# Two layers of each kind: five engine programs with a depth loop over a register, or written out one behind the other

## The chip, the cores and the metric

The kernel runs on one core of a Trainium2 chip. A core has five engines, each with its own instruction stream and its own sequencer: TensorE (PE; its weight loads are PEld), VectorE (DVE), ScalarE (ACT), GpSimd (POOL) and SyncE (SP), and 16 DMA engines that move data between device memory and on-chip memory. The engines meet only through semaphores: an instruction can wait until a semaphore has a value, and can raise one when it ends. The metric is the device time of one execution in microseconds; lower is better.

## The reference

A transformer of four layers on one sequence of 512 tokens with 1024 channels, in fp32: two layers of a first kind, then two of a second kind.

```python
def first_block(x, c, ...):
    c_act = silu(c)
    for l in range(DEPTH):                     # DEPTH = 2
        sh1, sc1, g1, sh2, sc2, g2 = split(c_act @ w_ada[l] + b_ada[l], 6)
        h = rms_norm(x, norm1_g[l]) * (1 + sc1) + sh1
        x = x + g1 * token_mixer(h, ...)       # gated linear attention + differential attention
        h = rms_norm(x, norm2_g[l]) * (1 + sc2) + sh2
        x = x + g2 * hier_moe(h, ...)          # 32 experts, 2 for each token
    return x

def second_block(x, ...):
    for l in range(DEPTH):
        h = _rmsnorm(x, norm1_g[l])
        q, k, v, su, sv, cb, cc, cx = split(h @ w_in[l])
        mix = concatenate([attention(rope(q), rope(k), v), spatial_gating(su, sv, sg_norm_g[l], ...), conv(cb, cc, cx)])
        x = x + mix @ w_out[l]
        h2 = _rmsnorm(x, norm2_g[l])
        gate, val = split(_dwconv3(h2 @ ffn_w_up[l], ffn_conv_w[l]))
        x = x + (silu(gate) * val) @ ffn_w_down[l]
    return x

def reference(...):
    return second_block(first_block(...), ...)
```

## The kernel before

Each engine has a program of its own: SyncE (line 570 on), GpSimd (677), TensorE (879), VectorE (1500) and ScalarE (2109). The five programs have the same shape. After a setup comes a loop over the two layers of the first kind, then one over the two layers of the second kind. These ten loops are `Fori(0, DEPTH)`: the layer `l` is a register, the body stands once in the instruction memory, and a branch at its end leads back. They begin at lines 615 and 647 (SyncE), 745 and 839 (GpSimd), 920 and 1277 (TensorE), 1520 and 1941 (VectorE), 2122 and 2340 (ScalarE).

The residual `xT` stays on chip, channels on the partitions. SyncE streams the weights into a ring of six slots of 4096 columns (`s_ring`). Matmuls with split weights run three times: ScalarE copies the high part of the weights and of the activations (`copy`, line 2112), GpSimd makes the low part of the weights (lines 767 and 860), VectorE the low part of the activations. All TensorE products are recorded by the helper `mm`, line 882. The small transfers of gains and tables are GpSimd's `small`, line 743. In the second half of each layer of the first kind, pairs of experts run in a second loop inside the first, over a number of pairs `ahead` that is read from memory (lines 641, 823, 1264, 1922, 2336). In a pass of it six transfers of 2048 KB bring the weights of two experts.

The order of work on each engine is that of its program, and the waits say how far the others must be. Every semaphore is counted up over the whole kernel: a helper `at(l, n)` gives the value for the n-th event of layer `l`, `l * per + n`. In a loop over a register that is a sum with a register in it, so a register step (ALU_OP in the trace, REGISTER_ALU in the compiled order) stands ahead of the instruction that waits. The engine's own chains are written with a helper too: `link` (lines 1945 to 1949) lets the next VectorE operation wait for the one before.

At the start of a layer of the second kind ScalarE squares the eight tiles of `xT` (line 2352), VectorE adds the squares one by one (`add_square`, below; its addition is line 1972, the register step of its wait line 1971), TensorE sums over the partitions with a matrix of ones, and the norm follows (lines 1955 to 1960). The layer ends with eight additions to `xT` on VectorE (line 2102), each released by a matmul.

```python
def add_square(squares, norm, k):
    ve.wait_ge(x_squared_b.sem, x_squared_b.at(l, KD * norm + k + 1))
    ins = ve.tensor_tensor(squares[0], squares[0], squares[k], ALU.add)
    if k < KD - 1:
        link(ins)
```

Of the kernel before, what the change touches and what calls it, by code (L numbers as in the profile page):

```python
# [39 lines left out]
DEPTH = 2  # L40
# [283 lines left out]
def program(nc, ctx, inp, out):  # L324
# [137 lines left out]
    def sig(name, per, credit=0):  # L462
        return Signal(sem(name), per, credit)
# [14 lines left out]
    linkA, linkB = sig("a_vector_link", LINKS["A"]), sig("b_vector_link", LINKS["B"])  # L478
# [18 lines left out]
    head_normed = sig("a_head_normed", 16)  # L497
# [52 lines left out]
    def settle(eng):  # L550

        eng.sem_inc(settled, 1)
# [4 lines left out]
    def slot_view(s, k, n):  # L557
        return ring[:, s, 0:k * n].rearrange("p (k n) -> p k n", k=k)
# [4 lines left out]
    def flat(units):  # L563
        return units.rearrange("p a s -> p (a s)")

    def tok(t, n=1):
        return slice(t * P, (t + n) * P)
# [4 lines left out]
    @block.sync  # L572
    def _(sp):
        def kn(w, c0, n):
            return w.rearrange("(k p) n -> p k n", p=P)[:, :, c0:c0 + n]


        for t in range(NT):
            sp.dma_start(flat(hT[:, 2 * t:2 * t + 2]), inp["x"][0, tok(t), :]).then_inc(x_in[t], 16)
        sp.wait_ge(cells_zero, 1)  # L580

        def source_a(name, l):
            kind, j = name[0], name[1] if len(name) > 1 else 0
            if kind == "ada":
                return KD, 512, kn(inp["w_ada"][l], 512 * j, 512)
            if kind == "lr":
                return KD, 32, kn(inp["w_in"][l], C_LR, 32)
            if kind in ("ya", "yb"):
                return 4, D, kn(inp["w_branch_a" if kind == "ya" else "w_branch_b"][l], 0, D)
            if kind == "wo":  # L590
                return KD, 512, kn(inp["w_out"][l], 512 * j, 512)
            c = {"gqk": 0, "gv": C_GV, "gg": C_GG, "dq": C_DQ, "dk": C_DK, "dv": C_DV, "ga": C_GA, "gb": C_GB}[kind]
            return KD, 512, kn(inp["w_in"][l], c + 512 * j, 512)

        freed_in_m = (m_in_read[0], m_in_read[1], m_down_made)

        last_of_high = {3: ("wo", 7), 4: ("wo", 3), 5: ("wo", 7)}

        def expert(l, number, e, u, layer_first, pieces=range(3)):

            for j in pieces:
                s = 3 * u + j
                if layer_first:

                    sp.wait_ge(TA.done.sem, TA.done_at(l, RA.reader_last(s) if s < 3 else last_of_high[s]))
                    settle(sp)

                sp.wait_ge(freed_in_m[j].sem, freed_in_m[j].at(number, u - 1))
                settle(sp)
                if j < 2:  # L610
                    sp.dma_start(slot_view(s, 4, D), kn(inp["w_expert_in"][l, e], 0, D)[:, 4 * j:4 * j + 4, :]).then_inc(weights_in_m[s], 16)
                else:
                    sp.dma_start(slot_view(s, 4, D), kn(inp["w_expert_out"][l, e], 0, D)).then_inc(weights_in_m[s], 16)

        with sp.Fori(0, DEPTH) as l:
            settle(sp)
            before = sp.value_load(cells[0:1, 0:1], min_val=0, max_val=BLOCKS)
            for name, *_ in RA.blocks:
                s = RA.slot(name)
                reader = RA.reader_before(name)  # L620
                if reader is None:

                    sp.wait_ge(freed_in_m[s % 3].sem, freed_in_m[s % 3].at(before * 2, s // 3 - 1))
                else:
                    sp.wait_ge(TA.done.sem, TA.done_at(l, reader))
                settle(sp)
                if name[0] == "rt":
                    v = slot_view(s, KD, 36)
                    sp.dma_start(v[:, :, 0:4], kn(inp["w_router_group"][l], 0, 4)).then_inc(weights_in_a[s], 16)
                    sp.dma_start(v[:, :, 4:36], kn(inp["w_router_expert"][l], 0, 32)).then_inc(weights_in_a[s], 16)  # L630
                else:
                    k, n, src = source_a(name, l)
                    sp.dma_start(slot_view(s, k, n), src).then_inc(weights_in_a[s], 16)

            for u, pieces in ((0, (1,)), (1, (1,)), (1, (0, 2)), (0, (2, 0))):
                expert(l, before * 2, u, u, True, pieces)
            sp.wait_ge(routed.sem, routed.at(l, 1))
            settle(sp)
            ahead = sp.value_load(cells[0:1, 1:2], min_val=NEXP // 2 - 1, max_val=BLOCKS // 2 - 1)

            with sp.Fori(0, ahead) as pair:
                for u in range(2):
                    e = sp.value_load(block_expert[0:1, bass.ds(2 * pair + (2 + u), 1)], min_val=0, max_val=NEXP - 1)
                    expert(l, before * 2 + (2 * pair + 2), e, u, False)

        total = sp.value_load(cells[0:1, 0:1], min_val=0, max_val=BLOCKS)
        with sp.Fori(0, DEPTH) as l:
            for name, *_ in RB.blocks:
                s = RB.slot(name)
                reader = RB.reader_before(name)  # L650
                if reader is None:
                    sp.wait_ge(freed_in_m[s % 3].sem, freed_in_m[s % 3].at(total * 2, s // 3 - 1))
                    settle(sp)

                    sp.wait_ge(TB.done.sem, l * TB.done.per + (TB.index[RB.reader_last(s)] + 1))
                else:
                    sp.wait_ge(TB.done.sem, TB.done_at(l, reader))
                settle(sp)
                j = name[1]
                if name[0] in ("in", "wo"):  # L660
                    src = inp["w_in_2" if name[0] == "in" else "w_out_2"][l]
                    sp.dma_start(slot_view(s, KD, 512), kn(src, 512 * j, 512)).then_inc(weights_in_b[s], 16)
                elif name[0] == "up":
                    i, n = UPS[j]
                    v = slot_view(s, KD, 2 * P * n)
                    for c in range(2):
                        sp.dma_start(v[:, :, P * n * c:P * n * c + P * n], kn(inp["ffn_w_up_2"][l], DFF * c + P * i, P * n)).then_inc(weights_in_b[s], 16)
                else:
                    sp.dma_start(slot_view(s, KF, P), kn(inp["ffn_w_down_2"][l], P * j, P)).then_inc(weights_in_b[s], 16)
        for t in range(NT):  # L670

            sp.wait_ge(out_copied, 2 * (t + 1))
            sp.dma_start(out[0, tok(t), :], flat(hT[:, 2 * t:2 * t + 2])).then_inc(out_stored, 16)
        sp.wait_ge(out_stored, 16 * NT)
# [3 lines left out]
    def _(pool):  # L678
# [63 lines left out]
        def small(signal, dst, src):  # L742
            pool.dma_start(dst, src).then_inc(signal.sem, signal.more(16))

        with pool.Fori(0, DEPTH) as l:
            settle(pool)
            before = pool.value_load(cells[0:1, 0:1], min_val=0, max_val=BLOCKS)
            for key, src, k in (("b_ada", rows(inp["b_ada"][l]), 48), ("n1", rows(inp["norm1_g"][l]), 8), ("n2", rows(inp["norm2_g"][l]), 8),
# [87 lines left out]
                for c in range(2):  # L836
                    small(y_loaded[t % 2], y01[t % 2][c], ys_rows[c * SEQ + t * P:c * SEQ + (t + 1) * P, :])

        with pool.Fori(0, DEPTH) as l:

            pool.wait_ge(TB.done.sem, l * TB.done.per + (TB.index[("par", 1)] + 1))
            settle(pool)
# [37 lines left out]
    def _(pe):  # L880
# [36 lines left out]
            last.then_inc(setup_p, 1)  # L917
        pe.wait_ge(setup_a, 1 + HEADS)

        with pe.Fori(0, DEPTH) as l:  # L920

            pe.wait_ge(TA.freed["V"].sem, TA.freed["V"].at(l, 0))
            settle(pe)
# [350 lines left out]
                done(last)  # L1274


        with pe.Fori(0, DEPTH) as l:
            pe.wait_ge(TB.freed["V"].sem, TB.freed["V"].at(l, 0))

            def opened(name):  # L1280
# [220 lines left out]
    def _(ve):  # L1501
# [15 lines left out]
        ve.wait_ge(setup_v, 11)  # L1517
        ve.memset(sc[:, 39:40], 0.0).then_inc(TA.freed["V"].sem, 1)

        with ve.Fori(0, DEPTH) as l:  # L1520
            linkA.given = 0

            def link(ins):
                ins.then_inc(linkA.sem, linkA.more())
# [413 lines left out]

        ve.wait_ge(TA.freed["V"].sem, DEPTH * TA.freed["V"].per + 1)
        ve.memset(sc[:, 39:40], 0.0).then_inc(TB.freed["V"].sem, KD)  # L1940
        with ve.Fori(0, DEPTH) as l:
            linkB.given = 0

            def link(ins):
# [165 lines left out]
    def _(ae):  # L2110
# [8 lines left out]
            ae.wait_ge(setup_p, 10 + h)  # L2119
            copy(U[:, 8 + 2 * h:10 + 2 * h], psum[:, 2 * h:2 * h + 2, :]).then_inc(setup_a, 1)  # L2120

        with ae.Fori(0, DEPTH) as l:
            settle(ae)
            before = ae.value_load(cells[0:1, 0:1], min_val=0, max_val=BLOCKS)

# [211 lines left out]
                pair(before * 2 + 2 * g, before + g, True)  # L2337
            pair(before * 2 + ahead * 2, before + ahead, False)

        with ae.Fori(0, DEPTH) as l:  # L2340
            def done(name):
                ae.wait_ge(TB.done.sem, TB.done_at(l, name))
                return psum[:, TB.bank(name), :]
# [72 lines left out]
            for j in range(PAIRS + 3):  # L2416
                if j < PAIRS:
# [3 lines left out]
                    for c in range(2):  # L2421
# [3 lines left out]
                        s = 160 + 8 * (i % 2) + 2 * t + c  # L2425
# [77 lines left out]
    for s in (TA.done, TB.done, *TA.freed.values(), *TB.freed.values(), params_in, router_bias_in, mod_ready, x_squared, root_taken,  # L2503
              h_scaled, h_ready, z_negabs, z_log, decay_summed, decay_exp, keys_queries_decayed, end_keys_made,
              head_squared, head_normed, lambda_dots, lambda_exp, max_negated, exps_made, weights_made, router_exp,
              router_diff, selected, routed, more_blocks, y_summed, h_high_a, h_low_a, weights_high_a, weights_low_a, params_in_b,
              tables_in, h_made_b, h_high_b, weights_high, weights_low, x_squared_b, squares_added, root_taken_b, inverse_made, h_low_b,
              head_squared_b, query_made, sv_squared, sv_mean, sv_normed, max_negated_b, sums_inverted, gated, convolved,
              mix_high, mix_low, up_centre, up_silu, hidden_made, hidden_high, hidden_low):
        assert s.given == s.per, (s.sem, s.given, s.per)  # L2510


# ---- launch: one core; inputs and output as the reference has them, and tables of the shapes
# [22 lines left out]
```

## Time and profile before

| | us |
|---|---|
| median of 3 runs | 3569.62 |
| lowest, highest | 3568.64, 3570.05 |
| the profiled execution's own time | 3567.01 |
| its span in the trace | 3565.3 |
| first boundary between layers of one kind (first kind) | about 1155 |
| second boundary (second kind) | about 2931 |
| mean granted TensorE clock | 0.934 |

Times in the profile count from the start of the span. Rows of a timeline give start, length, engine, line, operation, what it writes and reads, how many, and in brackets the engine's idle time before it and what ended that. An engine with a q behind its name (DVEq, PEldq) is the engine's sequencer: its branch, register and wait instructions. "issue" is time in which an engine waited for nothing that the profile shows. In a table of windows, each engine's busy time in the stretch is followed by its number of instructions in parentheses; the last three columns are the granted TensorE clock, the DMA engines' mean busy share, and GB/s.

### The profile page before, as it was taken

To read this page: it belongs to the slowest core of one execution; us is meant where nothing else is said; L and a number is where in the kernel's file an instruction comes from. 1 tells how busy PE (TensorE), PEld (TensorE's weight loads), DVE (VectorE), ACT (ScalarE), POOL (GpSimd) and SP (SyncE) were. 2 spreads that over 40 slices of the span, in tenths; PEclk is the share of its full clock that TensorE was granted. 3 is DMA by queue.
4 is the path that set the end of the run, shared out by engine and by line. 5 is a ranking of instruction groups with operands and counts; after the bars stand their busy time and mean duration, and the time that the engine had idled before them with its cause. 6 is when DMAs were issued, how large, how long until landed. Compare 5 with 4: busy or idle time off the path is not lost. (4 is left out here: it accounts for less than half of the span.)

```text
span 3565.3 us, 43004 instructions
## 1 busy us (share of the span) xinstructions
PE 3057.5 (86%) x14995; PEld 2020.6 (57%) x14995; DVE 1138.9 (32%) x2053; ACT 999.8 (28%) x1381; POOL 958.2 (27%) x886
## 2 busy tenths in 40 slices
PE   6988987888874798988888788498899989889999
PEld 4775675333332576656533333265788776568877
DVE  4365333111111446433211111234343313434331
ACT  4324332111110523432111111134333323433331
POOL 3412230111111322132111111231344443134443
PEclk7999997999997899999799999789999999999999
DMA  6214424999998212433599999611122341112232
GB/s 218 71 58 148 147 71 182 397 409 408 409 407 314 72 48 103 155 118 143 230 407 408 409 409 406 257 54 48 48 95 90 87 128 54 48 48 95 87 89 72
DMA packets 289712, 663.69 MB, mean 186 GB/s; under 512 B 20190, under 2 KB 114708, under 8 KB 289552
## 3 DMA queue, kind: packets, MB, share of 16 engines
q1 hardware_dynamic: 271680, 623.43, 46.8%
q0 software_dynamic: 17872, 38.14, 3.0%
q8 instruction: 98, 1.61, 0.2%
q14 instruction: 62, 0.51, 0.0%
HBM read 653.64 MB, written 25.69 MB: 191 GB/s over the span
## 5 line engine op out<-in xcount | busy, mean ns | idle before, releaser
L882 PE MATMUL psum<-s_parts 128*128 128x512 f32 (+1 forms) x4000 | 1010.0, 404 | 95.1 <-ACT s_parts L2112 44.4
L882 PEld LDWEIGHTS psum<-s_parts 128*128 128x128 f32 (+1 forms) x4000 | 764.6, 193 | 303.4 <-issue 43.8
L882 PE MATMUL psum<-s_ring,s_units 128*64 128x512 f32 x3168 | 745.0, 619 | 132.9 <-DMA s_ring<-in_w_expert_in 93.8
L860 POOL TENSOR_TENSOR s_parts<-s_ring,s_parts 128x512 fp32r<-128x512 f32 x368 | 468.9, 1311 | 756.4 <-ACT s_parts L2112 756.4
L882 PEld LDWEIGHTS psum<-s_ring,s_units 128*64 128x64 f32 x3168 | 248.4, 142 | 585.8 <-issue 450.3
L882 PE MATMUL psum<-s_h_low,s_parts 128*128 128x512 f32 (+1 forms) x2000 | 499.3, 390 | 1.7 <-DVE s_hid_low L2083 1.4
L767 POOL TENSOR_TENSOR s_parts<-s_ring,s_parts 128x512 fp32r<-128x512 f32 (+1 forms) x210 | 270.7, 1327 | 682.1 <-ACT s_parts L2112 682.1
L882 PEld LDWEIGHTS psum<-s_h_low,s_parts 128*128 128x128 f32 (+1 forms) x2000 | 372.9, 187 | 91.2 <-issue 9.1
L882 PE MATMUL psum<-s_units 128*128 (+9 forms) x1520 | 282.3, 401 | 61.3 <-DVE s_gsl L1859 24.7
L2112 ACT ACTIVATE s_parts<-s_ring 128x4096 fp32r<-128x4096 f32 (+3 forms) x80 | 259.0, 3240 | 177.2 <-PE psum L882 99.3
L882 PEld LDWEIGHTS psum<-s_units 64*128 64x128 f32 (+3 forms) x1520 | 174.6, 193 | 135.0 <-issue 104.3
L809 POOL DMA_INDIRECT s_units<-h_scratch,s_take_at x66 | 82.5, 1251 | 596.8 <-DVE s_take_at L1853 473.3
L1858 DVE TENSOR_SCALAR s_put_at<-psum,s_half_row 128x1 int32<-128x1 f32 x66 | 14.4, 218 | 705.2 <-DMA ys_scratch<-s_units,s_put_at 705.2
L2112 ACT ACTIVATE s_units<-psum 128x512 f32<-128x512 f32 (+1 forms) x264 | 152.0, 599 | 261.7 <-PE psum L882 224.8
L2092 DVE SCALAR_TENSOR_TENSOR s_units<-psum,s_par,s_units 128x511 f32<-128x511 f32 x88 | 66.0, 750 | 280.0 <-ACT s_units L2488 280.0
L818 POOL DMA_INDIRECT ys_scratch<-s_units,s_put_at x66 | 67.2, 1018 | 321.2 <-ACT s_units L2326 286.5
L2488 ACT ACTIVATE s_units<-psum,s_par 128x512 f32<-128x512 f32 x88 | 60.7, 690 | 307.6 <-PE psum L882 307.6
L2326 ACT ACTIVATE s_units<-psum,s_gsl 128x512 f32<-128x512 f32 x66 | 45.4, 687 | 359.0 <-PE psum L882 359.0
L882 PE MATMUL psum<-s_hid_low,s_parts 128*128 128x512 f32 x480 | 120.9, 389 | 0.0
L2320 ACT ACT_TABLE_LOAD x31 | 39.8, 1283 | 274.5 <-PE psum L882 274.5
L882 PEld LDWEIGHTS psum<-s_hid_low,s_parts 128*128 128x128 f32 x480 | 90.1, 188 | 18.8
L1538 DVE RECIPROCAL s_temps<-s_temps 128x512 f32<-128x512 f32 x28 | 93.9, 3353 | 19.5 <-ACT s_temps L2137 19.5
(354 smaller groups left out, 2505.2 us busy)
## 6 DMA issues: line engine op xcount, KB each, us to landing
s_ring<-in_w_expert_in SPq DMA_DIRECT2D x132, 2048.0 KB
s_ring<-in_w_expert_out SPq DMA_DIRECT2D x66, 2048.0 KB
s_ring<-in_w_in SPq DMA_DIRECT2D x28, 2048.0 KB, 8.7
s_ring<-in_w_ada SPq DMA_DIRECT2D x24, 2048.0 KB, 8.3
s_ring<-in_ffn_w_up SPq DMA_DIRECT2D x40, 1024.0 KB, 6.5
s_ring<-in_ffn_w_down SPq DMA_DIRECT2D x16, 1408.0 KB, 7.0
s_ring<-in_w_out SPq DMA_DIRECT2D x8, 2048.0 KB, 9.0
s_units<-ys_scratch POOLq DMA_DIRECT2D x16, 512.0 KB, 6.5
```

The costliest lines, as they stand in the source:

```text
L767: ins = pool.tensor_tensor(parts[:, s, cols], ring[:, s, cols], parts[:, 4 + n % 2, cols].bitcast(F32), ALU.subtract)
L809: pool.indirect_dma_start(out=xs[u % 2], out_offset=None, in_=h2_dram[:, :], in_offset=bass.IndirectOffsetOnAxis(ap=take_at[:, u % 2, 0:1] ...
L818: pool.indirect_dma_start(out=ys_dram[:, :], out_offset=bass.IndirectOffsetOnAxis(ap=put_at[:, u, 0:1], axis=0), in_=ys[u], in_offset=None ...
L860: ins = pool.tensor_tensor(parts[:, s, cols], ring[:, s, cols], parts[:, 4 + n % 2, cols].bitcast(F32), ALU.subtract)
L882: return pe.matmul(o, lhsT=lhsT, rhs=rhs, start=start, stop=stop)
L1538: link(ve.reciprocal(temps[:, 2, :], temps[:, 3, :]))
L1858: ve.tensor_scalar(put_at[:, u % 2, :], psum[:, 7, 1:2], 2.0, half_row[:, 0:1], ALU.mult, ALU.add).then_inc(m_put_written.sem, m_put_writt ...
L2092: link(ve.scalar_tensor_tensor(out=up_t[:, b, 1:SEQ], in0=o[:, 0:SEQ - 1], scalar=w[0], in1=up_t[:, b, 1:SEQ], op0=ALU.mult, op1=ALU.add))
L2112: return ae.activation(o, i, ACT.Copy) if scale is None else ae.activation(o, i, ACT.Copy, scale=scale)
L2320: ae.activation(sil[u], psum[:, u, 0:256], ACT.Silu).then_inc(m_silu_made.sem, m_silu_made.more())
L2326: ae.activation(ys[u], psum[:, 5 + u, :], ACT.Copy, scale=gsl[:, u:u + 1]).then_inc(m_ys_made.sem, m_ys_made.more())
L2488: ae.activation(up_t[:, n % 4, :], o, ACT.Copy, scale=par[:, col:col + 1]).then_inc(up_centre.sem, up_centre.more())
```

## The change

In all five programs `Fori(0, DEPTH)` becomes a Python `range(DEPTH)`. The body is written into the instruction stream twice, one copy behind the other, with `l` a constant 0 and then 1; the value in each wait is a constant, and the branch at the end of the body and the register steps of the waits are gone. The loops over `ahead` remain loops over a register, each of them now there twice. The host-side counts that are set back for each body (`given`) are adjusted. What is computed, the order of it on each engine, the tiles and the transfers are the same.

```diff
-        with sp.Fori(0, DEPTH) as l:
+        for l in range(DEPTH):
             settle(sp)
             before = sp.value_load(cells[0:1, 0:1], min_val=0, max_val=BLOCKS)
...
-        with pool.Fori(0, DEPTH) as l:
+        for l in range(DEPTH):
...
-        with pe.Fori(0, DEPTH) as l:
+        for l in range(DEPTH):
             pe.wait_ge(TB.freed["V"].sem, TB.freed["V"].at(l, 0))
...
-        with ve.Fori(0, DEPTH) as l:
-            linkA.given = 0
+        for l in range(DEPTH):
+            linkA.given = head_normed.given = 0
...
-        with ve.Fori(0, DEPTH) as l:
+        for l in range(DEPTH):
             linkB.given = 0
...
-        with ae.Fori(0, DEPTH) as l:
+        for l in range(DEPTH):
...
-        assert s.given == s.per, (s.sem, s.given, s.per)
+        assert s.given == (s.per if s is head_normed else DEPTH * s.per), (s.sem, s.given, s.per)
```

(Each of the loop lines stands twice in the kernel, once for each kind of layer; ten in all.)

In the compiled order of VectorE the second kind's loop looked like this at its two ends, before; the brackets say which semaphores an instruction waits for, and UNCONDITIONAL_BRANCH and COMPARE_AND_BRANCH are the loop's branches.

```order
L1940 MEMSET s_sc 128x1 [waits a_freed_by_vector]
L1941 UNCONDITIONAL_BRANCH
L1941 ISA
L1972 TENSOR_TENSOR s_units<-s_units 128x512 [waits b_x_squared]
L1946 ISA
L1971 REGISTER_ALU [waits b_vector_link]
L1972 TENSOR_TENSOR s_units<-s_units 128x512 [waits b_x_squared]
L1946 REGISTER_ALU
L1971 REGISTER_ALU [waits b_vector_link]
...
L2102 TENSOR_TENSOR s_xT<-psum,s_xT 128x512 [waits b_tickets_done]
L1941 REGISTER_ALU
L1941 COMPARE_AND_BRANCH
```

Now the end of the first copy and the head of the second stand next to each other, on VectorE:

```order
L2102 TENSOR_TENSOR s_xT<-psum,s_xT 128x512 [waits b_tickets_done] x8
L1972 TENSOR_TENSOR s_units<-s_units 128x512 [waits b_x_squared]
L1972 TENSOR_TENSOR s_units<-s_units 128x512 [waits b_x_squared,b_vector_link] x2
L1972 TENSOR_TENSOR s_units<-s_units,s_temps 128x512 [waits b_x_squared,b_vector_link] x4
L1981 COPY s_par<-psum 128x88 [waits b_tickets_done]
```

The branch between the residual's last update and the first addition is gone, and so are the register steps between the additions; the wait for `b_vector_link`, which a register step carried, stands on the addition itself, which now has two.

On ScalarE, in the attention of the second kind, line 2426 is the exponential of a tile of logits; a register step ahead of each carried one of its waits before:

```order
L2420 REGISTER_ALU
L2423 REGISTER_ALU [waits b_negated_max]
L2426 ACTIVATE s_units,s_lamv<-psum,s_lamv 128x512 [waits b_tickets_done]
L2423 REGISTER_ALU
L2426 ACTIVATE s_units,s_lamv<-psum,s_lamv 128x512 [waits b_tickets_done]
L2112 ACTIVATE s_units<-psum 128x4x128 [waits b_tickets_done]
```

and now the same exponentials are:

```order
L2426 ACTIVATE s_units,s_lamv<-psum,s_lamv 128x512 [waits b_tickets_done,b_negated_max]
L2426 ACTIVATE s_units,s_lamv<-psum,s_lamv 128x512 [waits b_tickets_done]
L2112 ACTIVATE s_units<-psum 128x4x128 [waits b_tickets_done]
```

Three register steps are gone and the first exponential carries both waits; nothing changed its place. Of an instruction with more than one wait, one stands on it and the others on a bare wait instruction ahead of it (EVENT_SEMAPHORE in the trace).

In all, the compiled programs have this many rows with a register step, and with a register step that carries a wait:

| engine | register steps before, after | of sequencer rows, carrying a wait, before, after |
|---|---|---|
| TensorE | 499, 22 | 146, 20 |
| VectorE | 800, 20 | 238, 80 |
| ScalarE | 414, 22 | 67, 22 |
| GpSimd | 57, 16 | 9, 12 |
| SyncE | 59, 6 | 68, 12 |

## Rows read from the trace of the kernel before

**Rows 1.** Page, section 1: busy time, share of the span, instructions.
```profile
PE 3057.5 (86%) x14995; PEld 2020.6 (57%) x14995; DVE 1138.9 (32%) x2053; ACT 999.8 (28%) x1381; POOL 958.2 (27%) x886
```

**Rows 2.** Windows: an expert stage, and the last layer between its boundaries.
```profile
640.00:1080.00 440.00, 365.59 (x1742) 148.56 (x1738) 53.36 (x167) 63.41 (x99) 63.51 (x56) 0.97 1.02 407
...
2935.00:3560.00 625.00, 582.44 (x2666) 456.73 (x2666) 222.46 (x316) 208.90 (x275) 227.84 (x182) 0.97 0.23 71
```

**Rows 3.** Back branches by line (duration ns min/median/max, first to last start); page, section 3.
```profile
L1941 DVEq COMPARE_BRANCH  x2: 49/56/63, 2931.2 to 3555.7; - x2
...
L920 PEldq COMPARE_BRANCH  x2: 86/2138/4190, 1147.2 to 2298.2; - x2
...
L1277 PEldq COMPARE_BRANCH  x2: 83/1726/3368, 2927.0 to 3551.5; - x2
...
L1264 PEldq COMPARE_BRANCH  x31: 76/208/256, 636.1 to 2235.3; - x31
...
q8 instruction: 98, 1.61, 0.2%
```

**Rows 4.** Chain of waits, 2925 to 2945 us (start us, us, what).
```profile
2925.00 6.13 PE psum L882 x27
...
2931.30 3.65 issue
...
2935.06 0.70 DVE s_units L1972
...
2935.79 0.04 DVEq L1971
...
2935.88 0.70 DVE s_units L1972
...
2940.70 1.88 PE psum L882 x8
```

**Rows 5.** Timeline at the first entry to the second kind and at its boundary.
```profile
2307.76 2.32 DVE L1972 TENSOR_TENSOR s_units<-s_units 128x512 f32<-128x512 f32 x3 [1.22 <-ACT s_units L2352]
...
2931.88 0.63 ACT L2352 ACTIVATE s_temps<-s_xT 128x512 f32<-128x512 f32 x1 [8.41 <-DVE s_xT L2102]
...
2955.12 10.32 POOL L860 TENSOR_TENSOR s_parts<-s_ring,s_parts 128x512 fp32r<-128x512 f32 x8 [20.95 <-ACT s_parts L2112]
...
2971.83 2.07 PE L882 MATMUL psum<-s_temps,s_aT 128*128 128x512 f32 x2 [5.75 <-DMA s_units<-in_sg_norm_g]
```

**Rows 6.** Timeline at the boundary between the two layers of the first kind.
```profile
1146.97 8.36 DVE L1935 SCALAR_TENSOR_TENSOR s_xT<-psum,s_mod,s_xT 128x128 f32<-128x128 f32 x32
...
1156.28 10.05 PE L882 MATMUL psum<-s_hT,s_ones 128*128 128x512 f32 x16 [7.42 <-ACT s_hT L2133]
```

**Rows 7.** Sequencer instructions by line: register steps and bare waits.
```profile
L1971 DVEq ALU_OP  x26: 40/40/40, 2308.5 to 3180.4; - x26
...
L1294 PEldq EVENT_SEMAPHORE  x74: 51/51/51, 2316.1 to 3540.2; - x74
...
L552 DVEq EVENT_SEMAPHORE  x102: 21/21/21, 143.0 to 1737.5; - x102
```

**Rows 8.** Timeline of the router and of an exponential; chain of waits in attention.
```profile
582.33 0.17 DVE L1769 TENSOR_REDUCE s_units<-s_units 128x4 f32<-128x16 f32 x1
582.53 0.18 DVE L1770 TENSOR_TENSOR s_units<-s_units 128x16 f32<-128x16 f32 x1
...
2451.81 0.78 ACT L2426 ACTIVATE s_units<-psum,s_lamv 128x512 f32<-128x512 f32 x1 [0.85 <-PE psum L1428]
...
3036.17 0.04 ACT s_units L2426
...
3036.74 0.04 ACTq L2342
```

**Rows 9.** Chain of waits, 2935 to 3560 us: its shares by line.
```profile
by line: PE psum L882 79.8%; issue 3.3%; POOL s_parts L860 2.1%; PE psum L1428 1.7%; DVE s_hid_low L2083 1.5%; ACT s_parts L2112 1.5%; ACT s_units L2426 1.2%; DMA s_ring<-in_ffn_w_down 1.1%; ACT s_units L2112 1.0%; DVE s_units L1972 1.0%; D
```

**Rows 10.** Windows behind the second kind's boundary; the third last column is the granted clock.
```profile
2940.70:2946.80 6.10, 3.94 (x16) 3.56 (x16) 2.15 (x8) 0.83 (x2) 0.00 (x0) 0.50 0.01 4
```

More of the change, by code:

```diff
@@ L646, in _ @@
         total = sp.value_load(cells[0:1, 0:1], min_val=0, max_val=BLOCKS)
-        with sp.Fori(0, DEPTH) as l:
+        for l in range(DEPTH):
             for name, *_ in RB.blocks:
@@ L837, in _ @@
                     small(y_loaded[t % 2], y01[t % 2][c], ys_rows[c * SEQ + t * P:c * SEQ + (t + 1) * P, :])
-        with pool.Fori(0, DEPTH) as l:
+        for l in range(DEPTH):
             pool.wait_ge(TB.done.sem, l * TB.done.per + (TB.index[("par", 1)] + 1))
@@ L1274, in _ @@
                 done(last)
-        with pe.Fori(0, DEPTH) as l:
+        for l in range(DEPTH):
             pe.wait_ge(TB.freed["V"].sem, TB.freed["V"].at(l, 0))
@@ L2120, in _ @@
             copy(U[:, 8 + 2 * h:10 + 2 * h], psum[:, 2 * h:2 * h + 2, :]).then_inc(setup_a, 1)
-        with ae.Fori(0, DEPTH) as l:
+        for l in range(DEPTH):
             settle(ae)
@@ L2338, in _ @@
             pair(before * 2 + ahead * 2, before + ahead, False)
-        with ae.Fori(0, DEPTH) as l:
+        for l in range(DEPTH):
             def done(name):
```

## Prediction

> **What bounds the kernel now.** I read the page first: TensorE is busy for 86% of the span [rows 1]. That is an average over stages, so the table of stages came second [rows 2]. In the expert stage the 16 DMA engines are full (share 1.02, 407 GB/s) and TensorE works 365.59 of 440 us: the stream of weights sets the pace there. In the second layer of the second kind TensorE works 582.44 of 625 us and the DMA engines only 0.23 of the time: matmuls set the pace, and what can still be won is the 43 us in which TensorE stands still, at the places where a chain of small operations on VectorE, ScalarE and GpSimd has to finish before the next matmul. The change touches only sequencers: the loop's branches, and register steps that work out what value a wait is for. So the third question was where a sequencer is what the others wait for. For that I read the branch and register instructions by line, then the chain of waits and the timeline at the two places where a layer follows another of its kind.
>
> **The back branches.** Each engine has two depth loops and takes one back branch in each. I looked at what comes behind each branch and who waits for it.
>
> *VectorE at the second kind's boundary.* The COMPARE_BRANCH itself lasts 49 to 63 ns [rows 3], but the chain of waits has 3.65 us of "issue" behind it, from 2931.30 to 2934.95, and only then the loop head's register step and, at 2935.06, the first addition of squares [rows 4]. What that addition needs was there long before: its operands' last writer on VectorE had ended, and ScalarE writes the last of the eight squares at 2931.88 to 2932.51 [rows 5]. Where the same code is entered without a back branch, the first addition starts at 2307.76, and the 1.22 us ahead of it are put down to ScalarE's square, not to issue [rows 5]. The profile's third section lists a queue of kind "instruction", 1.61 MB in 98 packets [rows 3], so code is fetched in pieces of 16 KB while the kernel runs; I take the gap for such a fetch. Seven additions of 0.70 us follow, each with some 0.11 us ahead of it, and TensorE stands still until 2940.70, when the last is done [rows 4]. So this gap is on the path, wholly. Unrolled, the next layer's code lies right behind. The additions can then start at about 2931.9, when the last update of the residual is done, and they are as long as before; the first seven squares are long done and the eighth comes at 2932.5, far ahead of the addition that uses it. TensorE's sums start at 2937.5 in place of 2940.7. **−3.2 us.** Next late is the same chain of additions, since nothing else arrives between: TensorE's own back branch, at 2927.0, is over at 2930.4 [rows 3]. Behind it the shift must survive two more hand-overs. GpSimd's low parts at 2955.12 wait for ScalarE, which waits for this layer's normed input; and the gating norm's weights, sent by GpSimd after those, release TensorE at 2971.83 [rows 5]. Both hang on the same chain and move with it, so I take nothing off.
>
> *The others.* TensorE's back branches are the long ones, 4190 ns at 1147.2 and 3368 ns at 2927.0 [rows 3]. Both lie beside other work. At 1147.2 TensorE has queued matmuls of the final sum; it could use new code only when VectorE's 32 updates (1146.97 to 1155.33) and ScalarE's squares are there, at 1156.28, 4.9 us after the branch came back [rows 6]. At 2927.0 its queue held matmuls until 2931.1 [rows 4]. VectorE's own branch in the first kind is queued right behind those updates, and its sequencer runs ahead of them by a few instructions; ScalarE's next work is released by the updates' end and by nothing later: free. If the cover were gone, each would cost its 3 to 4 us. I count 0 for all of them.
>
> The Trainium skill ("Runtime: NRT & Kernel Launch", section on instruction fetch mechanics) says that a taken branch to code outside the current two pages stops the engine until the page has come, and that straight code crosses page ends nearly for free. By that rule every one of these back branches costs a fetch; this case's trace agrees for VectorE and TensorE, but shows only one of them with an engine waiting for it, so by the rule alone the sum would be some 11 us (three gaps of 3.4 to 4.2 us), by the rows it is 3.2.
>
> **The register steps.** With the layer in a register each wait's value is worked out by an ALU_OP ahead of it, 40 ns on VectorE [rows 7]. Counted in the compiled programs, such rows fall from 800 to 20 on VectorE, 414 to 22 on ScalarE, 499 to 22 on TensorE. Three cases:
>
> 1. The step stands behind an instruction that is still running, and costs nothing. This is the usual one. In the router's chain VectorE's small operations of 0.17 to 0.18 us follow each other after 0.03 us with a register step between each two [rows 8]. On ScalarE, in attention, an exponential starts at 3036.17 and the last register step (ACTq) behind it ends at 3036.78; such an exponential takes 0.78 us, which covers it [rows 8].
> 2. The step itself carries a wait (an operation that waits for two semaphores puts the first on the register step), as in the additions: 0.70, then 0.03 + 0.04 + 0.04 [rows 4]. In the changed program 238 → 80 such rows remain on VectorE, but the first wait does not go: what carries it is then a bare EVENT_SEMAPHORE, 21 ns on VectorE but 51 ns on TensorE, whose register step takes 32 ns [rows 7]. The gain is 19 ns a time on VectorE, and on TensorE a loss of 19 ns where it is exposed.
> 3. The step stands on a sequencer that has just been released. It costs its 0.04 us and perhaps as much again of issue.
>
> Bounds: nothing at all on the one side. On the other, if all 238 carrying rows of VectorE lay on the path in both layers, 238 × 2 × 0.019 = 9 us less; if all 146 of TensorE did, 146 × 2 × 0.019 = 5.5 us more. The chain of waits tells which end is nearer: in the whole second layer of the second kind I count 17 VectorE, 31 ScalarE and 15 GpSimd or SyncE steps on it, 0.7, 1.2 and 0.5 us (the first addition's and the exponential's are two of them [rows 4, 8]). ScalarE's are in the shadow of case 1. Of the other 1.2 us I let half go, 0.6 us a layer; the first kind has somewhat more of them, and its chain can't be followed, so 0.7 us a layer as an estimate. 2 × 0.6 + 2 × 0.7 = **−2.6 us**.
>
> **At nothing.** The expert stage: full DMA engines hide all that its sequencers do, and its loops stay loops. The reads of cells stay. Table loads are the same in number. The start of a layer's transfers moves by under 0.1 us an issue.
>
> **Sum.** −3.2 − 2.6 = −5.8 us. The profiled execution took 3567.01 us beside a span of 3565.3 and a median of 3569.62. Its own time would become 3561.2; the median **3563.8 us**. The clock leaves ±1.7 us: TensorE's granted clock is 0.50, its lower level of 1.2 GHz, from 2940.70 on, after the standstill [rows 10], and a standstill of 5.2 us in place of 8.4 may let it fall less, or just so, since it also falls at the 5.75 us gap before 2971.83.
>
> **Rivals.**
> - *The register steps are worth more.* Case 3 is more frequent than the chain shows, above all in the first kind. At all of VectorE's bound, −9 − 3.2 gives 3557; with plain steps exposed as well, 3554. For it: 3.3% of the last layer's chain, 20 us, are "issue" [rows 9]. Against: most of that is shadow of work that runs. Chance 0.27.
> - *Nothing comes of it.* The fetch gap is still there (straight code must be fetched too, VectorE's additions begin right at a new page), or its 3.2 us are lost again in the low clock or at GpSimd. 3567 to 3570. For it: 3.2 us are less than 0.1%. Against: nowhere inside a layer do I see a gap of 3 us put down to issue on a waiting engine. Chance 0.2.
> - *Slower: the expert loops are moved in the code.* They stay loops but exist twice, at other addresses. Now their 31 back branches cost TensorE 76 to 256 ns, with no fetch [rows 3]. If a copy's body lies so that its head is no longer at hand, each costs a fetch of 4.2 us. TensorE's cover is (440 − 365.59) us over the pairs of that stage. A pair of experts moves six transfers of 2048 KB, 30.9 us at 407 GB/s, so 14.2 pairs, 5.2 us each. One fetch fits. It decides from a stall of 5.2 us, as where two pages miss in each pass: 8.4 − 5.2 = 3.2 us over 31 passes is 99 us, 3663 us; in one of the two copies, some 3615. Chance 0.05.
> - *TensorE's bare waits are exposed*: 5.5 us more against 5.8 less, no change, 3569. Chance 0.04, in "same".
>
> The likeliest, my forecast's own case, has 0.44, with a range of 3561 to 3567.
>
> **How the numbers follow.** About 0.2%, 7.1 us, is what a measurement of this kernel can tell from no change: faster is under 3562.5, slower over 3576.8. Most of the first rival and a fourth of my own case lie under 3562.5: 0.37. The slower rival and an odd change of placement: 0.07. The rest, 0.56. The range reaches from the large register gain, 3554, to just above no change, 3571.
>
> **What would show it.** Right: at the second kind's boundary the first addition of squares starts within 0.1 us of VectorE's last update, TensorE's ones matmuls 3.2 us earlier relative to that update, and TensorE's idle time there is 5.2 us; the gaps between additions go from 0.11 to about 0.09 us; the first kind's boundary keeps its 7.4 us. Wrong: a gap of issue behind any of the former loop ends, back branches of the expert loops over 0.3 us, an expert stage longer by more than 1 us, or long stages of matmuls that changed their length, which no step of mine would explain.

## The result, and the profile after

The changed kernel took 3579.13 us (median of 6 runs, 3571.19 to 3589.28) against 3569.13 us; the ratio is 1.0027, interval [1.0015, 1.004]: 9.6 us slower, where 5.8 us faster was forecast. The profiled execution has a span of 3574.0 us beside 3565.3. Its page begins like that of before [rows 1], with fewer instructions and a little more TensorE time:

```profile
span 3574.0 us, 39482 instructions
...
PE 3065.4 (86%) x14995; PEld 2025.2 (57%) x14995; DVE 1144.1 (32%) x2053; ACT 999.8 (28%) x1381; POOL 956.7 (27%) x886
```

**The gap that was to go is gone.** The chain of waits of the changed kernel at the second kind's boundary (start us, us, what):

```profile
2934.68 0.04 DVE s_xT L2102
2934.71 0.57 issue
2935.28 0.70 DVE s_units L1972
2935.98 0.02 issue
2936.00 0.70 DVE s_units L1972
...
2940.38 1.65 PE psum L882 x7
```

In [rows 4] there were 3.65 us of issue behind the last update of the residual; now the first addition starts 0.57 us behind the record of that update, when its execution is over. From the update to TensorE's first sum it is 2940.38 − 2934.68 = 5.70 us, before 2940.70 − 2931.16 = 9.54 us: −3.84 us. Between additions there are 0.02 us where [rows 4] have 0.11; the register step is gone, and what stands between two additions is a bare wait instruction, which doesn't appear in the chain:

```profile
L1971 DVEq EVENT_SEMAPHORE  x14: 21/21/21, 2313.4 to 3186.4; - x14
```

**The expert loops cost no fetch, and their stage is as it was** [rows 2, 3]; back branches by line, and a window of the first expert stage:

```profile
L1264 PEldq COMPARE_BRANCH  x31: 83/215/249, 628.2 to 2230.7; - x31
```

```profile
640.00:1080.00 440.00, 362.89 (x1730) 146.78 (x1728) 53.48 (x167) 63.16 (x98) 63.51 (x56) 0.97 1.03 408
```

**Two new stalls stand elsewhere.** The first lies where the first kind ends and the second begins. Timeline of the changed kernel:

```profile
2288.32 1.23 DVE L1928 TENSOR_TENSOR s_units<-s_units 128x1024 f32<-128x1024 f32 x1 [4.96 <-DMA s_units<-ys_scratch]
...
2291.61 0.52 POOL L743 DMA_DIRECT2D s_prow<-in_conv_w  x1
2291.62 11.41 DVE L1928 TENSOR_TENSOR s_units<-s_units 128x1024 f32<-128x1024 f32 x1 [2.07 <-DMA s_units<-ys_scratch]
2292.14 9.80 POOL L860 TENSOR_TENSOR s_parts<-s_ring,s_parts 128x512 fp32r<-128x512 f32 x8
...
2303.17 1.94 PE L1273 MATMUL psum<-s_ident,s_units 128*128 128x128 f32 x8 [11.54 <-DVE s_units L1928]
```

and of the kernel before, the same place:

```profile
2293.04 1.23 DVE L1928 TENSOR_TENSOR s_units<-s_units 128x1024 f32<-128x1024 f32 x1 [5.09 <-DMA s_units<-ys_scratch]
...
2296.57 1.23 DVE L1928 TENSOR_TENSOR s_units<-s_units 128x1024 f32<-128x1024 f32 x1 [2.30 <-DMA s_units<-ys_scratch]
2297.00 0.52 POOL L743 DMA_DIRECT2D s_prow<-in_conv_w  x1
2297.54 2.62 POOL L860 TENSOR_TENSOR s_parts<-s_ring,s_parts 128x512 fp32r<-128x512 f32 x2
...
2297.94 1.30 PE L1273 MATMUL psum<-s_ident,s_units 128*128 128x128 f32 x5 [1.59 <-DVE s_units L1928]
```

Line 1928 is VectorE's sum of the two experts' outputs of 128 tokens. The last of four took 11.41 us in place of 1.23. Beside it GpSimd makes the second kind's first low part, eight subtractions without a gap, 9.80 us. They end at 2301.94, the sum 1.09 us later: that is nearly its whole ordinary length, so it did hardly anything before they were over. TensorE waited 11.54 us for the sum in place of 1.59. Matched event by event, the changed kernel was 4.6 us ahead of the kernel before at VectorE's second last product of the experts (line 1864, 2244.25 against 2248.85), and 5.2 us behind at the copy that follows the sum (2302.95 against 2297.71): 9.8 us lost here.

The second stall is in attention. ScalarE in the changed kernel:

```profile
3081.04 1.28 ACT L2449 ACT_TABLE_LOAD   x1
...
3082.33 0.20 ACT L2449 ACTIVATE s_lamv<-s_lamv 128x4 f32<-128x4 f32 x1
...
3089.15 1.28 ACT L2426 ACT_TABLE_LOAD   x1 [6.62 <-PE psum L1428]
...
3090.45 0.78 ACT L2426 ACTIVATE s_units<-psum,s_lamv 128x512 f32<-128x512 f32 x1
...
3092.71 1.72 PE L882 MATMUL psum<-s_ident,s_lamv 128*64 128x128 f32 x16 [3.20 <-ACT s_units L2112]
```

and in the kernel before:

```profile
3078.33 1.28 ACT L2449 ACT_TABLE_LOAD   x1
...
3079.62 0.21 ACT L2449 ACTIVATE s_lamv<-s_lamv 128x4 f32<-128x4 f32 x1
3079.85 1.28 ACT L2426 ACT_TABLE_LOAD   x1
...
3086.55 0.78 ACT L2426 ACTIVATE s_units<-psum,s_lamv 128x512 f32<-128x512 f32 x1 [5.42 <-PE psum L1428]
...
3088.72 1.09 PE L882 MATMUL psum<-s_ident,s_lamv 128*64 128x128 f32 x16 [1.77 <-ACT s_units L2112]
```

The square root of line 2449 needs another table than the exponentials, so a table load of 1.28 us brings the exponential's back. Before, it ran at 3079.85, in 6.7 us in which ScalarE waited for logits. Now it runs when the logits are there, 1.30 us ahead of the exponential, and TensorE stands still for 3.20 us in place of 1.77. The same is seen in the layer before, at 2464.16. In the changed kernel TensorE then works at its lower level for a while. Windows just behind that restart, of the changed kernel and of the kernel before; the third last column is the granted clock:

```profile
3092.70:3096.30 3.60, 3.59 (x20) 1.83 (x20) 1.80 (x5) 3.60 (x2) 0.00 (x0) 0.55 0.00 0
```

```profile
3088.70:3092.00 3.30, 3.28 (x25) 2.16 (x26) 2.02 (x6) 3.30 (x2) 0.00 (x0) 1.00 0.00 0
```

Over the last layer, from TensorE's first sum of squares to the first matmul of line 1497, the same 2635 matmuls keep TensorE busy for 586.71 us in the changed kernel and for 578.84 us in the kernel before:

```profile
2940.40:3565.10 624.70, 586.71 (x2635) 458.70 (x2635) 212.84 (x304) 208.82 (x275) 227.90 (x182) 0.96 0.22 69
```

```profile
2940.70:3556.40 615.70, 578.84 (x2635) 453.26 (x2635) 214.65 (x304) 208.90 (x275) 227.84 (x182) 0.97 0.22 68
```

### The profile page after: what moved, and what is told of

The parts are those of the page before. It is cut to its first block and busy times, and to the rows that moved or that the text cites. A ratio compares the mean times of both kernels' runs of the same rounds, so it can differ in the third digit from the quotient of the medians.

```text
span 3574.0 us, 39482 instructions
## 1 busy us (share of the span) xinstructions
PE 3065.4 (86%) x14995; PEld 2025.2 (57%) x14995; DVE 1144.1 (32%) x2053; ACT 999.8 (28%) x1381; POOL 956.7 (27%) x886
```

## The experiments

Each was timed against the kernel before on the same chip; the microseconds behind a ratio are the ratio's distance from 1 times 3570.

**GpSimd's first low part held back.** In the changed kernel, ahead of `low_part(0)`:

```diff
+            if l == 0:
+                pool.wait_ge(y_summed.sem, y_summed.at(DEPTH - 1, NT))
             low_part(0)
```

> The changed kernel, with one more wait: ahead of GpSimd's first low part of the second kind (the eight subtractions that began at 2292.14 us in the changed kernel's trace) it waits for VectorE's four residual sums of the experts' outputs. Theory A (GpSimd's eight subtractions shut out VectorE's last sum, which took 11.41 us in place of 1.23): that sum takes 1.2 to 1.8 us, the handover from the first kind to the second is about 10 us earlier than in the changed kernel, and the time falls by about 10 us, to about 3569, or less against the kernel before (ratio 0.998 to 1.000), with a narrower spread than the changed kernel's 18 us. Rival B (the loss is in lower TensorE clock and scattered, the long sum is a single execution's accident or only shows what waited anyway): the median stays within 3 us of 3579.

Measured: 3568.15 us, ratio 0.9993 [0.9984, 1.0001], −2.5 us, 12 us under the changed kernel. All eight sums of line 1928 take 1.22 to 1.23 us. The spread stayed wide (3561.56 to 3576.39), against what theory A expected: the shutting out alone doesn't make it. Rival B falls.

**The collision without the change.** The kernel before, its low part moved ahead of the ten small loads:

```diff
+            low_part(0)
             pool.wait_ge(TB.done.sem, l * TB.done.per + (TB.index[("par", 1)] + 1))
...
-            low_part(0)
```

> The kernel before, its loops over a register as they were, with GpSimd's first low part of the second kind moved ahead of its ten small loads of gains, so that its eight subtractions begin at about 2291 us, before VectorE's last sum (2296.57) is released. Theory A: the last one or two sums are shut out until the subtractions end at about 2301, so that the first kind ends 3 to 5 us later (2301 + 1.2 against 2297.8), and the trace shows a sum of 4 to 11 us; the whole is slower by 3 to 8 us. Rival B: sums of 1.23 to 1.8 us, and no change of the time.

Measured: 3573.89 us, ratio 1.0013 [1.0004, 1.0021], +4.6 us. Its timeline (lines 848 and 1927 are 860 and 1928 of the kernel before):

```profile
2293.55 9.79 POOL L848 TENSOR_TENSOR s_parts<-s_ring,s_parts 128x512 fp32r<-128x512 f32 x8
2294.96 10.61 DVE L1927 TENSOR_TENSOR s_units<-s_units 128x1024 f32<-128x1024 f32 x2 [5.12 <-DMA s_units<-ys_scratch]
2303.30 1.62 POOL L743 DMA_DIRECT2D s_prow<-in_ffn_conv_w  x3
```

The two last sums together take 10.61 us; one of them alone 9.47. Here GpSimd's eight subtractions began 1.4 us ahead of the sum. The stall needs no written-out layers, only GpSimd being early.

**Each kind alone.** The depth loops of the second, or of the first kind, put back in all five programs:

```diff
-        for l in range(DEPTH):
+        with ve.Fori(0, DEPTH) as l:
```

> Only the first kind's layers written out; the second kind's loops are over a register as before. Theory A: the first kind gains what it gained in the changed kernel (8 to 10 us by 1140 us, 4 us at the end of its second layer), GpSimd comes to its low part about as early as in the changed kernel (its small loads keep two of their register steps, some 0.5 us), so the long sum may or may not be there: 3565 without it, 3575 with it. The fetch gap of 3.65 us at 2931 is there. Rival C (written-out code costs by itself, in the second kind): 3562 to 3566, clearly under the kernel before, without a change at the handover.

> Only the second kind's layers written out; the first kind's loops as before. Theory A: no register steps between GpSimd's small loads, so it comes to its low part 0.6 us earlier relative to VectorE's last sum, as in the changed kernel; the sum is shut out in some or all executions: 3570 to 3577; the gap at 2931 is gone (-3.2 us). Rival B (clock, scattered): the second layer of the second kind is 3 to 9 us longer by stretches at half clock, 3570 to 3575 with a sum of 1.23 us. Rival C: nothing but -3.2 us, 3566.

Measured: first kind alone 3569.48 us, ratio 0.9992 [0.9981, 1.0002], sums of 1.22 us; second kind alone 3584.27 us, ratio 1.0039 [1.0025, 1.0053], +14 us, with a sum of 11.39 us and the late table loads. That is more than the 3570 to 3577 us that were expected. All of the loss came with the second kind.

**The table load brought forward.** In the changed kernel, behind the square root; and the same with the wait of the first experiment:

```diff
                     ae.activation(few[:, 20:24], few[:, 16:20], ACT.Sqrt).then_inc(root_taken_b.sem, ...)
+                    ae.activation(few[:, 28:29], few[:, 16:17], ACT.Exp)
```

> The changed kernel with the one-column exponential of e6_both alone. Theory D: 5 to 7 us less than the changed kernel's 3579 to 3581, ratio to the kernel before about 1.001 to 1.0015, and the long sum of about 11.4 us at the handover still there. Rival E: ratio 1.0027 as the changed kernel's.

> The changed kernel with the wait of e1_order, and with one exponential of a single column more on ScalarE, right behind the square root of line 2449, in each layer of the second kind; it writes a cell that nobody reads and brings the table load ahead of the wait for the logits. Theory D (the table load of 1.28 us that the changed program has behind the wait for the logits, at 2464.16 and 3089.15 us, is on the path, and the longer standstill of TensorE there drops its clock each time): 2.6 to 3.6 us a layer, 5 to 7 us in all, come back on top of e1_order's 3568; I expect 3562 to 3564, ratio 0.9975 to 0.998, and TensorE's idle time there 1.8 us in place of 3.2. Rival E (the exponentials wait for something else anyway, and the loss in the second kind is the clock's own scatter): the same as e1_order within 2 us.

Measured: the exponential alone 3571.54 us, ratio 1.0000 [0.9992, 1.0009], its long sum of 11.75 us still there; it gave back more than the 5 to 7 us that were expected, though within the two intervals. Both together 3562.18 us, ratio 0.9974 [0.9965, 0.9983], −9.3 us. ScalarE in that kernel (lines 2451, 2452, 2428 and 884 are 2449, the new exponential, 2426 and 882):

```profile
3080.40 1.28 ACT L2451 ACT_TABLE_LOAD   x1
...
3081.92 1.28 ACT L2452 ACT_TABLE_LOAD   x1
...
3088.54 0.78 ACT L2428 ACTIVATE s_units<-psum,s_lamv 128x512 f32<-128x512 f32 x1 [5.12 <-PE psum L1430]
...
3090.80 1.09 PE L884 MATMUL psum<-s_ident,s_lamv 128*64 128x128 f32 x16 [1.92 <-ACT s_units L2114]
```

The load stands in ScalarE's idle time again, and TensorE waits 1.92 us. The four side by side, each against the kernel before on its own chip:

| | table load late | table load early |
|---|---|---|
| GpSimd free to start | 1.0027, +9.6 us (the change) | 1.0000, 0 us |
| GpSimd waits for the sums | 0.9993, −2.5 us | 0.9974, −9.3 us |

The shutting out costs 12 or 9 us by the columns, the late table loads 10 or 7 us by the rows, each with some 5 us of uncertainty.

**Is it the sum's length?** Each sum of 1024 columns as two of 512:

```diff
-                ve.tensor_tensor(y01[t % 2][0], y01[t % 2][0], y01[t % 2][1], ALU.add).then_inc(...)
+                ve.tensor_tensor(y01[t % 2][0][:, 0:512], y01[t % 2][0][:, 0:512], y01[t % 2][1][:, 0:512], ALU.add)
+                ve.tensor_tensor(y01[t % 2][0][:, 512:1024], ...).then_inc(...)
```

> The changed kernel with each of VectorE's sums of 1024 columns (line 1928) written as two of 512. In the kernel before's trace VectorE operations of 512 columns and GpSimd's subtractions take turns (1.73 and 1.77 us each), while the sum of 1024 columns was shut out for the whole train of eight. Theory A1 (a train of GpSimd operations without a gap shuts out any VectorE operation with two inputs from SBUF that comes while it begins): no change, 9 to 11 us lost on one of the two halves, ratio 1.0027. Theory A2 (only the long operation is shut out; a short one gets its turn behind the GpSimd operation that runs): the two halves take at most 1.8 us each, some 8 us less than the changed kernel, ratio about 1.0005.

Measured: 3577.15 us, ratio 1.0012 [1.0000, 1.0024]. The interval touches the changed kernel's, so the time tells little; the trace does: the first half is shut out for the whole train.

```profile
2293.33 10.59 DVE L1928 TENSOR_TENSOR s_units<-s_units 128x512 f32<-128x512 f32 x1 [2.15 <-DMA s_units<-ys_scratch]
2293.57 9.80 POOL L860 TENSOR_TENSOR s_parts<-s_ring,s_parts 128x512 fp32r<-128x512 f32 x8
2303.84 0.68 DVE L1929 TENSOR_TENSOR s_units<-s_units 128x512 f32<-128x512 f32 x1
```

**Is it the idle time ahead of it?** In the changed kernel, ahead of the last sum alone:

```diff
+                if l == DEPTH - 1 and t == NT - 1:
+                    ve.memset(sc[:, 38:39], 0.0)
```

> The changed kernel with a fill of one column on VectorE directly ahead of the last sum of line 1928 alone; the fill takes the wait for the data, and the sum follows it with no idle time between. Where VectorE and GpSimd took turns in the kernel before, VectorE's operation followed another of its own; the sums that were shut out came after 2 us of idle time. Theory F (an operation that comes behind VectorE's own work gets its turn): the sum takes 1.2 to 3 us and some 8 us come back, ratio 1.000. Rival G (the idle time doesn't matter): the sum again takes 10 us or more, ratio 1.0027.

Measured: 3580.46 us, ratio 1.0034 [1.0021, 1.0047]; the sum took 11.88 us. The fill lasts 0.06 us and reads nothing from SBUF, so by itself it is a weak test of theory F. The trace of the kernel before has a stronger one: after 9.82 us of idle time a VectorE subtraction with two SBUF inputs came in the middle of a GpSimd train and took 0.71 us, and the GpSimd subtraction behind it 1.73 in place of 1.27.

```profile
57.51 0.71 DVE L1587 TENSOR_TENSOR s_h_low<-s_hT,s_parts 128x512 fp32r<-128x512 f32 x1 [9.82 <-ACT s_parts L2112]
```

Idle time alone does not make the shutting out; theory F falls.

**Controls, and what is left of the change.**

> The kernel before with the wait of e1_order ahead of GpSimd's first low part in each layer of the second kind. In the kernel before the last sum took 1.23 us and GpSimd began 0.97 us behind it. If the kernel before never meets the shutting out, no change (ratio 0.9995 to 1.0005); if it meets it in some executions, the median may stay while the slowest executions go, and the wait gains up to 1 us.

> Only the second kind written out, with the wait ahead of GpSimd's first low part and with the one-column exponential. What is left of the change in the second kind is then the fetch gap (-3.2 us) and the register steps (-1.2 us by the prediction): 3567 to 3568 against 3571.8, ratio 0.9985 to 0.999. If written-out code cost anything else there, the ratio would be 0.9995 or more.

> Only the first kind written out, with the wait ahead of GpSimd's first low part. The prediction gave the first kind 1.4 us. e6_both, at 9.3 us under the kernel before, leaves some 5 us for it: ratio 0.9985 by that, 0.9996 by the prediction.

> The kernel of e6_both once more, unchanged. Its ratio was 0.9974 (-9.3 us), while its two halves, e9_second_both and e10_first_order, came to 1.0000 and 0.9992, 3 us together. If the halves add up, this comes out at 0.999; if e6_both's value holds, at 0.9965 to 0.9983.

Measured: the wait in the kernel before 3571.39 us, ratio 0.9996 [0.9987, 1.0005]: no sign that the kernel before meets the stall. Second kind with both repairs 3570.30 us, 1.0000 [0.9991, 1.0009], where 0.9985 to 0.999 was expected; first kind with the wait 3567.68 us, 0.9992 [0.9983, 1.0001]; both kinds with both repairs, again, 3561.42 us, 0.9974 [0.9962, 0.9985]. The halves come to 0 and −2.9 us, the whole twice to −9.3. With intervals of ±3 us on each half this is a gap of 6 us, at or just beyond the edge of what chance allows; how much each kind gives stays open. The second kind's zero is a miss that stands: by the measure set for it ahead of the run, 0.9995 or more means that something else in its written-out code costs time. The interval reaches down to −3 us, so this isn't shown either. The whole is firm, and it is the best version: 0.26% under the kernel before.

## Why the prediction was wrong

**What held.** The fetch gap at 2931 was on the path and is gone: −3.2 forecast, −3.84 in the trace, of which some 0.6 are the additions' register steps. That is the gain at this place. Whether it reaches the end is not shown: from TensorE's first sum of the second kind's first layer to the first matmul of line 1497 behind the second layer the traces have 1240.6 to 1243.6 us in the five kernels with the second kind's loop, and 1237.2 to 1244.3 us in the four that are written out with the table load early. Where the second kind is still a loop, the gap stays; the chain of the kernel with the first kind alone and the wait (line 1942 is 1941 of before):

```profile
2930.33 0.06 DVEq L1942
2930.39 3.81 issue
2934.20 0.06 DVEq L1942
```

The back branches beside other work cost nothing, the first kind's boundary kept its standstill (TensorE 7.26 us, before 7.42 [rows 6]), and the expert stages did not slow down, so the slower rival (a fetch at every back branch of the expert loops) falls: 83 to 249 ns against 76 to 256.

**A term mis-sized.** For a register step that carries a wait I gave 19 ns, the difference of two instructions' lengths [rows 7]. In the one chain where it can be read, it is 0.09 us: what stands on the bare instruction is now the wait that has long been satisfied, and it runs in the shadow of the operation ahead; the late one stands on the operation itself. Between two additions the gap went from 0.11 to 0.02 us. With both stalls repaired the change gives −9.3 us [−12.5, −6], where the sum said −5.8; that the register steps give the rest is not shown, since the halves do not add up to the whole.

**The step that failed is the part "At nothing", twice.**

1. "Table loads are the same in number." They are, but not in the same place. Before, the wait for the row maxima stood on a register step and the table load behind it carried no wait for logits. Now the exponential has both waits with no register step ahead, and the load that is put ahead of it carries the one for the logits. The compiled order shows it on ScalarE, before:

```order
L2449 ACTIVATE s_lamv<-s_lamv 128x4 [waits b_sv_mean]
L2420 REGISTER_ALU
L2423 REGISTER_ALU [waits b_negated_max]
L2426 ACT_TABLE_LOAD
L2426 ACTIVATE s_units,s_lamv<-psum,s_lamv 128x512 [waits b_tickets_done]
```

and now:

```order
L2449 ACTIVATE s_lamv<-s_lamv 128x4 [waits b_sv_mean]
L2426 ACT_TABLE_LOAD [waits b_tickets_done]
L2426 ACTIVATE s_units,s_lamv<-psum,s_lamv 128x512 [waits b_negated_max]
```

1.30 us are its direct cost in each layer. By the traces most of what it costs is in the last layer: from TensorE's sum of squares (2940.70 before, 2940.38 after) to the first matmul of line 1497 (3556.39, 3565.10) it is 615.7 us before and 624.7 after. Over the profiles it is 615.7 to 617.3 in the five kernels that keep the second kind's loop, 621.5 to 624.7 in the five with the load late, and 615.7 to 619.9 in the four with it early. So some 5 to 7 us: 1.3 of the load, the rest time at the lower clock, since the same matmuls are busy for 578.8 to 581.1, 584.0 to 587.3 and 579.0 to 584.2 us in these three groups. That the longer standstill is what lowers the clock is read from the windows above; moving the load brought most of it back. In the layer ahead of it, from TensorE's first sum to its last matmul, no difference stands out of the scatter (615.2 to 621.7 us in all).

2. "The start of a layer's transfers moves by under 0.1 us an issue." True of each, and I called it nothing because it made things earlier. GpSimd issues ten small loads ahead of its first low part; they took 2297.52 − 2292.02 = 5.50 us and take 2292.13 − 2287.07 = 5.06, and another 0.37 us ahead of them are gone (`[0.37 <-issue]` in the trace of before). VectorE's last sum became earlier by less. So the eight subtractions came 0.52 us behind the sum's start in place of 0.97. More telling is when GpSimd's sequencer passed the wait that stands right ahead of them (in the helper `settle`, line 552; its sequencer's rows, of the changed kernel and of the kernel before):

```profile
L552 POOLq EVENT_SEMAPHORE  x1: 17/17/17, 2291.0 to 2291.0; - x1
```

```profile
L552 POOLq EVENT_SEMAPHORE  x1: 17/17/17, 2297.1 to 2297.1; - x1
```

In the loop a register step (line 856) stood ahead of that wait, and was passed only at 2297.0, when the last but one small load was over. Written out, that step is gone, and the sequencer is through the wait some 1.2 us ahead of the first subtraction in place of 0.5. So the subtractions were handed over before the sum started (2291.62), where before they came after it (2296.57). Every trace without the added wait divides by this order:

| kernel | GpSimd's sequencer past its wait | sum starts | sum's length |
|---|---|---|---|
| before | 2297.1 | 2296.57 | 1.23 |
| first kind alone | 2300.5 | 2300.24 | 1.23 |
| the change | 2291.0 | 2291.62 | 11.41 |
| second kind alone | 2304.5 | 2305.15 | 11.39 |
| table load early | 2301.4 | 2301.69 | 11.75 |
| halved sum | 2292.4 | 2293.33 | 10.59 |
| fill ahead of the sum | 2295.4 | 2295.57 | 11.88 |
| low part moved, kernel before | 2293.2 | 2294.96 | 9.47 |

This is eight traces that agree, not an experiment that moved the sequencer alone. The prediction asked what a late engine delays, never what an early one runs into.

The Trainium skill ("SBUF — State Buffer", section "Who interferes with whom") says that a VectorE instruction with two inputs in SBUF contends with a GpSimd instruction that reads SBUF, and that the order of issue decides which of the two is blocked. The contention agrees with the trace. So does the order, if it is taken where the sequencers hand over, as in the table; by the starts of the records it does not, since the sum's began 0.52 us ahead of the first subtraction's. How long the loser waits is for the trace to say: for all eight subtractions.

**What stays open.** Elsewhere in the same traces the two engines take turns: at 490.16 us of before a VectorE subtraction of 512 columns takes 1.78 us beside GpSimd ones of 1.73 and 1.75, and so again at 493.57 and 496.97. What decides between turns and being shut out for a whole train was not found: not the length (the halved sum), not the idle time ahead of it (the fill, and the row at 57.51). The distance from the sum's start to the train doesn't tell who wins either: with 0.72 and 0.97 us it went through (first kind alone, and before), with 0.87 and 0.99 it was shut out (early table load; fill); the sequencer's order in the table does. And the run-to-run spread is wider in several of the written-out kernels, with either kind alone (3558.70 to 3578.51 with the first, 3575.07 to 3596.34 with the second) and with both (3571.19 to 3589.28); no profile tells why.

## What to carry to other kernels

When an edit takes sequencer work away, list for every engine what starts earlier, its sequencer above all, and look at what runs beside it there: a GpSimd train that its sequencer has handed over before VectorE starts a sum with two SBUF inputs can cost its whole length, and one added wait on GpSimd prevents it. When waits move from separate instructions onto operations, look in the compiled order at which instruction now holds each wait, table loads above all; one dummy operation in idle time can put a load back. Write a layer loop out only with these two repaired: here that turned +9.6 us into −9.3 us.

## What the runs showed that I had not expected

- Whether VectorE's sum was shut out went, in eight traces, by whether GpSimd's sequencer had passed its wait before the sum started, and not by how far behind the sum GpSimd's first subtraction began.
- A VectorE operation of 0.69 us with two SBUF inputs took 10.59 us beside eight GpSimd subtractions, and one of 1.23 us up to 11.88 us.
- A standstill of TensorE of 3.20 us in place of 1.77 was followed by a granted clock of 0.55 against 1.00 over the matmuls behind it.
- A bare wait instruction, 21 ns on VectorE, costs nothing on the path when its semaphore is already there: additions 0.70 us long follow each other after 0.02 us.
